# Two transformer blocks in float32 on one core: the second block's residual held by features, its norm scales applied behind the matmuls

## The reference

```python
def rmsnorm(x, g):
    x32 = x.astype(jnp.float32)
    y = x32 * lax.rsqrt(jnp.mean(x32 * x32, axis=-1, keepdims=True) + RMS_EPS)
    return (y * g.astype(jnp.float32)).astype(x.dtype)

def swiglu(h, w_gate, w_up, w_down):
    return (jax.nn.silu(h @ w_gate) * (h @ w_up)) @ w_down

def second_block(x, norm_mix, norm_ffn, w_qkv_a, w_out_a, sink_a, w_qkv_b, w_out_b,
              w_gate, w_up, w_down, norm_final):
    for i in range(DEPTH_2):
        h = rmsnorm(x, norm_mix[i])
        j = i // 2
        if i % 2 == 0:
            x = x + window_gqa_sink(h, w_qkv_a[j], w_out_a[j], sink_a[j])
        else:
            x = x + dilated_mixture_attention(h, w_qkv_b[j], w_out_b[j])
        h = rmsnorm(x, norm_ffn[i])
        x = x + swiglu(h, w_gate[i], w_up[i], w_down[i])
    return rmsnorm(x, norm_final)
```

## Time and profile before

| | us |
|---|---|
| median of 3 runs | 1625.37 |
| lowest and highest run | 1621.87 and 1625.46 |
| span of the profiled execution | 1619.0 |
| TensorE busy in it | 1377.1 (85%) |
| VectorE busy | 611.9 (38%) |
| ScalarE busy | 478.8 (30%) |
| DMA, mean over the span | 232 GB/s |

### The profile page before, as it was taken

How to read it: one execution, slowest core, us unless ns; L and a number is a source line. 1 busy time by engine, 2 the same in 40 slices (tenths; PEclk the granted TensorE clock), 3 DMA queues, 4 the chain that set the end, 5 groups by cost and what they waited for, 6 DMA issues and landing times.

```text
span 1619.0 us, 21195 instructions
## 1 busy us (share of the span) xinstructions
PE 1377.1 (85%) x8730; PEld 995.8 (62%) x8730; DVE 611.9 (38%) x848; ACT 478.8 (30%) x698; POOL 104.1 (6%) x99
## 2 busy tenths in 40 slices
PE   5999899786655655655699999999999999999997
PEld 1478665531111101111397899998999988899996
DVE  3225636410100100100447545455444455564544
ACT  2423522310000000000344534444344443343443
POOL 0000011100000000000034000000000045100000
PEclk9999999796767767767799999999999999999999
DMA  8443618989999999999641555655666620256562
GB/s 342 151 117 85 226 42 320 409 322 409 410 410 410 410 410 410 409 410 410 226 143 54 157 181 182 195 170 167 193 185 185 181 89 14 78 153 186 170 205 66
DMA packets 136658, 376.08 MB, mean 232 GB/s; under 512 B 8312, under 2 KB 55849, under 8 KB 136400
## 3 DMA queue, kind: packets, MB, share of 16 engines
q1 hardware_dynamic: 134600, 372.89, 65.0%
q10 hardware_dynamic: 1992, 2.26, 0.4%
HBM read 374.07 MB, written 1.05 MB: 232 GB/s over the span
## 4 chain that ended last, share of the span: by engine, by line
PE 68%; DMA 18%; DVE 6%; SPq 5%; ACT 2%; issue 1%; DVEq 0%; ACTq 0%
PE psum L1738 15%; PE psum L1739 15%; PE psum L1740 15%; DMA ring<-in_w_up 6%; DMA ring<-in_w_down 6%; DMA work<-in_w_gate 5%; SPq L528 5%; PE psum L2025 4%; PE psum L2143 3%; PE psum L2110 2%; PE psum L2123 1%; PE psum L1900 1%; PE psum L2105 1%; PE psum L1759 1%; PE psum L1893 1%
## 5 line engine op out<-in xcount | busy, mean ns | idle before, releaser
L1738 PE MATMUL psum<-parts 128*128 128x256 f32 (+1 forms) x1520 | 466.8, 307 | 3.7 <-DVE parts L1471 1.9
L1739 PE MATMUL psum<-parts 128*128 128x256 f32 (+1 forms) x1520 | 466.1, 307 | 0.0
L1740 PE MATMUL psum<-parts 128*128 128x256 f32 (+1 forms) x1520 | 465.8, 306 | 0.0
L1426 DVE TENSOR_TENSOR parts<-ring,parts 128x1024 fp32r<-128x1024 f32 x232 | 282.5, 1226 | 219.5 <-ACT parts L962 219.5
L962 ACT CAST parts<-ring 128x1024 fp32r<-128x1024 f32 x232 | 241.0, 1047 | 277.1 <-PE psum L1740 242.4
L1738 PEld LDWEIGHTS psum<-parts 128*128 128x128 f32 x1520 | 290.3, 191 | 18.8 <-issue 3.3
L1740 PEld LDWEIGHTS psum<-parts 128*128 128x128 f32 x1520 | 290.3, 191 | 13.3
L1739 PEld LDWEIGHTS psum<-parts 128*128 128x128 f32 x1520 | 290.4, 191 | 12.9
L2025 PE MATMUL psum<-ring,work 128*32 128x512 f32 x512 | 90.6, 846 | 64.8 <-DMA ring<-in_w_up 32.7
L2025 PE MATMUL psum<-work 128*32 128x512 f32 x512 | 85.7, 812 | 41.5 <-DMA work<-in_w_gate 21.7
L952 ACT ACTIVATE work<-psum 128x1024 f32<-128x1024 f32 x4 | 4.1, 1024 | 389.5 <-PE psum L2025 389.5
(11 more groups left out here) (315 smaller groups left out, 1483.4 us busy)
## 6 DMA issues: line engine op xcount, KB each, us to landing
ring<-in_w_qkv_b SPq DMA_DIRECT2D x72, 512.0 KB, 3.7
work<-in_w_gate SPq DMA_DIRECT2D x16, 2048.0 KB, 23.8
ring<-in_w_up SPq DMA_DIRECT2D x16, 2048.0 KB, 24.0
ring<-in_w_ada SPq DMA_DIRECT2D x48, 512.0 KB, 8.5
work<-in_w_down SPq DMA_DIRECT2D x12, 2048.0 KB, 24.0
ring<-in_w_gate SPq DMA_DIRECT2D x44, 512.0 KB, 3.9
ring<-in_w_up SPq DMA_DIRECT2D x44, 512.0 KB, 4.6
ring<-in_w_down SPq DMA_DIRECT2D x44, 512.0 KB, 3.6
```

Source lines behind the costliest of these rows:

```text
L1426: dve.tensor_tensor(part_of(lo_slots, t, n), ring[:, slot_2(t), 0:n], part_of(hi_slots, t, n), ALU.subtract).then_inc(lo_ready, 1)
L1738: pe.matmul(out, lhsT[0], rhs[0], start=start, stop=False, skip_group_check=True)
L1739: pe.matmul(out, lhsT[0], rhs[1], start=False, stop=False, skip_group_check=True)
L1740: return pe.matmul(out, lhsT[1], rhs[0], start=False, stop=stop, skip_group_check=True)
```

## The change

The residual of the second block is now `xT`, the same memory as `xres`, with features on partitions and tokens in the order that attention wants (even tokens, then odd). No stage turns it. The norm's factor per token, `r`, is not applied to the activations: `h_hi` and `h_lo` are x times the gain alone, and `r` multiplies results: q and k when they leave PSUM, v per partition, and in the FFN both the gate sums (before SiLU) and the product. `r` itself comes from squares on ScalarE, a sum over the eight feature tiles on VectorE (a reduction whose inner index steps by 256 elements), a matmul with ones that sums over the partitions, root and reciprocal of 256 elements. Where tokens are on partitions (v), `r` is turned by two small matmuls (`r_to_tokens`). The two norms at the start are one pass: `r_one` of the first, `r_all` the product.

The output projections and the first FFN's down projection are by features now, and their sums join `xT` bank by bank (`grow`). The second FFN's down projection stays by tokens: 16 matmuls (`residual`) put the turned residual into its sums first, and the final norm reads PSUM. The experts' results are added by features, for which x is turned once behind the router's logits. The Q weights come before the K weights. Three, not two, weight tiles are split before a stage's residual is added.

```diff
-            turn(xn, xt_ready)
+            gate(5)
...
+            turn(xn, xt_ready, X_BANK)
...
+            turn(xres, xt_ready, X_BANK)
             pe.wait_ge(aff_ready, 1)
...
-            gate(5)
             pe.wait_ge(top_done, 1)
...
+            def sums_of_squares(m, n=L):
+                pe.wait_ge(sq_summed, m + 1)
+                pe.matmul(ps[0][:, 0:n], ones, sq_sum[:, 0:n], start=True, stop=True).then_inc(sums_out, 1)
+
+            def r_to_tokens(m):
+                pe.wait_ge(r_ready, m + 1)
                 for t in range(TT):
...
+                    ins = pe.matmul(ps[1][:, 2 * t:2 * t + 2], r_all[:, P * t:P * t + P], ident[:, 0:2], start=True, stop=True)
+                ins.then_inc(sums_out, 1)
...
+                for k in range(KD):
+                    if k % 2 == 0:
+                        pe.wait_ge(o_lo_ready, o_ready + k // 2 + 1)
+                    w = weights(t + k)
+                    for f in range(KD):
+                        ins = feature_sums(w, bank, f, k, k == 0, k == KD - 1)
+                        if k == KD - 1 and f in (1, 3, 5):
+                            ins.then_inc(first_sums, 1)
+                    ins.then_inc(tiles_done, 1)
...
+                    for j in range(2):
+                        w = weights(t + j, turn)
+                        for f in range(KD):
+                            ins = products(ps[f // 2][:, L * (f % 2):L * (f % 2) + L], each(w, slice(None), slice(P * f, P * f + P)),
+                                           each(hid, slice(None), j), first and j == 0 and f % 2 == 0, last and j == 1)
...
+                def residual():
+                    for p in range(TT):
+                        for f in range(KD):
+                            pe.matmul(ps[2 * p + f // 4][:, P * (f % 4):P * (f % 4) + P], xT[:, f, P * p:P * p + P],
+                                            ident[:, :], start=(f % 4 == 0), stop=False, skip_group_check=True)
...
+                if i == 1:
+                    pe.wait_ge(r_tok_ready, 2)
...
+            def grow_and_norm(n, bank, done, gain):
+                grow(n, bank, done, 0)
+                grow(n, bank, done, 1)
+                dve.wait_ge(x_grown, 4 * n + 1)
+                low_h(n + 1, gain, 0)
+                grow(n, bank, done, 2)
+                dve.wait_ge(x_grown, 4 * n + 2)
+                low_h(n + 1, gain, 1)
+                grow(n, bank, done, 3)
...
+            def over_features(i, sq):
+                return dve.tensor_reduce(sq_sum[:, L * i:L * i + L], sq.rearrange("p k l -> p l k"), AX.X, ALU.add)
...
+            def rows_of_r(m, n):
+                dve.wait_ge(sums_out, (2, 5)[n])
+                dve.tensor_copy(r_tok[:, :], ps[1][:, 0:2 * TT]).then_inc(r_tok_ready, 1)
...
+                def block_gate(ready, buf):
+                    dve.wait_ge(tiles_done, ready)
+                    dve.tensor_tensor(gated_r[:, buf].rearrange("p (j l) -> p j l", j=2),
+                                      ps[4 + 2 * buf].rearrange("p (j l) -> p j l", j=2), by_r(2), ALU.mult).then_inc(ff_gate, 1)
...
+            def squares():
                 act.activation(stats[:, 90:91], ident[:, 0:1], ACT.Sqrt)
...
+                    ins = act.activation(sq_x[:, 2 * b:2 * b + 2, :], xT[:, 2 * b:2 * b + 2, :], ACT.Square)
```

More of the change, by code:

```diff
@@ new lines, in _ @@
+            for k in range(4, KD):
+                split(T_QA + k)
+            root(0)
+            split(T_KA)
+            root(1)
+            for t in range(T_KA + 1, T_OA):
+                split(t)
+            act.wait_ge(k_n_spread, 1)
+            act.copy(k_a[:, 2:4, :], ps[1]).then_inc(k_a_ready, 1)
+            act.wait_ge(tiles_done, T_VA + 2)
+            act.wait_ge(r_tok_ready, 1)
+            for t in range(TT):
+                ins = act.activation(v_a[:, t, :], ps[3][:, L * t:L * t + L], ACT.Copy, scale=r_tok[:, 2 * t:2 * t + 1])
@@ L1077, in _ @@
+            ins.then_inc(v_a_ready, 1)
             attention(0, T_OA)
-            for k in range(2):
+            for k in range(3):
                 split(T_FF[0] + k)
-            rms(4, x_grown, 1)
-            split(T_FF[0] + 2)
-            scaled(1, C_FFN2, halves)
+            normed(cols[:, C_FFN2:C_FFN2 + KD], x_grown, 0)
+            split(T_FF[0] + 3)
+            squares().then_inc(squared, 1)
             ffn(0, T_QB)
-            rms(5, x_grown, TT + 1)
-            split(T_QB + 2)
@@ L1086, in _ @@
-            scaled(2, C_MIX2 + KD, even_odd)
-            for i in range(3 * GROUPS):
-                for k in range(3 if i == 0 else 0, KD):
+            normed(cols[:, C_MIX2 + KD:C_MIX2 + 2 * KD], x_grown, 4)
+            split(T_QB + 3)
+            squares().then_inc(squared, 1)
+            for k in range(4, KD):
+                split(T_QB + k)
+            root(3)
+            for i in range(1, 3 * GROUPS):
+                for k in range(KD):
                     split(T_QB + KD * i + k)
-                    if k == 2:
-                        proj_half(i - 1)
+                    if k == 2 and (i - 1) % 3 == 2:
+                        values_out(i - 1)
@@ L1093, in _ @@
             attention(1, T_OB)
[L1094 removed]
+            for k in range(3):
                 split(T_FF[1] + k)
[L1096 to L1098 removed]
+            normed(cols[:, C_FFN2 + KD:C_FFN2 + 2 * KD], x_grown, 8)
+            split(T_FF[1] + 3)
+            squares().then_inc(squared, 1)
             ffn(1, None)
[L1100 removed]
+            act.activation(stats[:, 90:91], ident[:, 0:1], ACT.Sqrt)
```

577 lines of the change are left out of this document (300 added, 277 removed).

## The result

The changed kernel takes 1643.71 us (median of 4, 1641.04 to 1647.73) against 1625.41 for the kernel before on the same chip: a ratio of 1.0122, interval 1.0101 to 1.0144. It is slower by 18 us where 8 us less was forecast, and lies outside the range of 1613 to 1626. The profiled execution of the changed kernel spans 1645.9 us.

A forecast was written before the change was run, and what follows sets the result against it. TensorE was taken to bound the second block, the experts' weights by DMA the time before 792 us. Terms -4.8 - 2.8 - 0.8 + 6.1 - 0.9 - 2.2 - 2.8 = -8.2 us gave 1617.2, range 1613 to 1626.

The forecast's parts named there:

- (f): Start of the second block: first matmul 7.9 us earlier, most given back, including 2.0 for uncovered softmax latency; -0.9 us.
- (g): Routing: FFN gate moved into an idle stretch, clock taken as held at 1.00, first new expert load earlier; -2.2 us.
- (i): Remaining edits priced at nothing, among them the experts' sums as 8 x 256 columns, under DMA but for the last.
- (a): Boundaries one to three: TensorE resumes 1.35 us after the last matmul instead of pausing 6.86; bounds 0 and 2.5.
- (b): Norm's scale beside the matmuls: reduction 2.2 us, reciprocal 1.6, about 0.55 lost to the ones matmul; boundary one -4.8 us.
- the rival of half-rate reads: Reduction's strided reads at half rate, 4.4 us, make weights' low halves late: 5.0 us, total 1622.2; chance 0.15.
- the third rival: The same reduction costs more, turning the kernel slower from 6 us; at 7.2 us +19, 1636; chance 0.07.
- (c): Boundary two pays 2.1 us for r in token order after the eighth tile, -2.8; boundary three adds the residual, -0.8.
- (d): Output projections and first FFN's down projection: 38 tiles of 24 narrower matmuls at 2.88 instead of 2.72 us; +6.1 us.
- (e): Inside the FFN: extra VectorE operations and SiLU's wait cost nothing, under a cover of 1.6 us per block.
- (h): Tail after the last matmuls: 5.95 us instead of 8.75, since the addition goes; -2.8 us.
- the first rival: The clock falls in the FFN gate at 297.7; routing +1.6 instead of -2.2, total 1621.0; chance 0.25.

The follow-up runs named there:

- experiments 1 to 3: Changed kernel, ten unused matmuls before attention: 1612.12 us; kernel before, scores behind second value tile: 1660.96 us profiled; changed kernel, twenty unused matmuls behind fourth attention unit: 1623.18 us.
- experiment 7: Changed kernel with the sums over feature tiles reading their elements in a row instead of 1 KB apart: 1.12 ns an element; no total time given.
- experiment 9: Changed kernel with scores earlier, large tiles aligned, x transposes later, three additions for the reduction, r turned after the sixth tile: 1596.59 us against 1625.59 before.
- experiment 6: Changed kernel with scores behind the second value tile's first quarter and work put back to 416 bytes past a multiple of 512: 1618.79 us against 1625.59 before.
- experiment 2: Kernel before with the first scores moved behind the second value tile: profiled 1660.96 us; other executions 1657.71, 1652.27 and 1626.27 us.

## Why the prediction was wrong, point by point

- **(f) is the step that failed.** It named the stretch ("no longer covers softmax latency, 2.0") and sized it well (2.32 us), but priced only the idle time. The clock's part is 32.6 us (experiments 1 to 3). Terms (f) and (g) did ask about the clock, at a cold start and at the gate; here it was not asked. From the earlier trace rows term (g) reads that in attention the clock "stays at 1.00 once there", and takes it as a comfort; the runs show that a fall stays too. No rival had this mechanism. The rest of (f) holds: 8.0 us sooner at the first matmul (7.9 forecast), 6.5 given back (7.0); the half clock lasts from the first matmul (793.6) to 798.0, which is worth some 2 us, as summed.
- **(i) was the second miss, the other way.** "At nothing" was said of the experts' stage after looking at its instructions. Two small tiles moved a large one, and the DMA rate went from 410 to 420 GB/s: -11.1 us in this stage, 10.0 of them between its first and last landing. Without it the changed kernel would be near 1655. No rival had it.
- **(a)** Pause at boundaries 1.67 us from start to start, so some 1.55 over the normal step, forecast 1.35, all three the same: right. The rival that pauses stay at 4 us has fallen.
- **(b)** The reciprocal takes 1.75 us (1.6 forecast). The reduction takes 3.93, not 2.2: the lower bound was taken, and the rival of half-rate reads had the better duration (4.4) at a price of 5.0 us. TensorE waited 0.43 us for it at three places, and 0.50 at the FFN's first output; FFN and boundary two together are 1.4 over the sum, where experiment 7 gives back 1.6. Replacing it in experiment 9, with the move at boundary two, was worth 5.2 us. The slower reductions of the third rival didn't occur.
- **(c)** The wait behind the eighth tile came as told, 1.54 us: VectorE's copy of r, then the split behind it. The stretch is 0.7 over. Here too the clock was not asked: it fell behind this wait in five of nine profiles, for 1.4 us each (experiment 6), though not in that of the result.
- **(d)** 2.88 to 2.89 us a tile, as forecast. **(e)** No wait of 0.5 us or more in the later blocks: hidden, as forecast. **(h)** FFN and tail come to +2.7 instead of +1.9.
- **(g)** The gate ran at full clock from 302.3 to 306.5, but the clock fell behind it, in the pause ahead of the normed tokens: the transposes take 3.32 us, the logits 5.07, the transposes of x 3.65. That is the first rival's mechanism, a step later. The gain of 2.2 is not there (+1.9 in this pair, none over all variants).
- **The sum without the two misses.** -8.2 forecast, -7.0 measured in experiment 6 (interval -3.9 to -10). The total agrees; its parts do so less. In the changed kernel's table the second block without the attention comes to -3.5 where its terms gave -6.0, and over all profiles routing gains nothing where (g) gave -2.2. So part of the agreement is luck.
- **The signs.** Two of the prediction's own signs of being wrong came true: the reduction takes over 3 us, and the first new load goes out at 345.7 (7.1 of that is the first stretch's spread). Neither is what made the kernel slower.
- **The 6.4 us** between the median and the span were chance: the profiled execution of the kernel before was a fast one. In the other runs the time and the span of one execution differ by 1.8 to 2.2 us.

## What to carry to other kernels

Before a cover is taken from an idle stretch of TensorE, ask what the clock does behind it: if narrow matmuls follow, a fall can be paid over all of them (here 32.6 us), and ten useless dense matmuls are cheaper (2.3 us). When a change adds or resizes any tile, compare the start addresses of the large tiles that DMA fills, modulo 256 bytes, and the GB/s of a full stage, before the difference is given to the change. Cut both traces at the same events and read the clock column of each stretch; busy shares hide a halved clock.

## What the runs showed of the hardware that was not expected

- TensorE idle for 2.20 to 2.33 us at clock 1.00 ahead of attention was followed by 0.50 in all five profiles with such a stretch; by its time, one unprofiled execution of experiment 2 escaped it. Attention's units stay at 0.50 for some 70 us, though TensorE is busy throughout; 20 matmuls of 512 columns lift the clock, and without them it rose in the last outputs or the turning of the results (918.1 in experiment 2, 910.7 in the changed kernel). The Trainium skill (TensorE: Matmul & The Clock Gate, HAM oscillation — how this bites in real kernels) describes the fall behind waits for DMA, ahead of matmuls that recover each time; here the work behind did not recover for 72 us.
- An idle stretch of 1.55 us between dense matmuls was followed by 3.4 us at 0.50 in five of nine profiles, one of 1.85 us in none of four.
- 2 MB in rows of 4 KB from DRAM: 5.12 us if the rows start 128 or 416 bytes past a multiple of 512 in SBUF, 4.85 to 5.02 at a multiple of 256. With work and early alone well placed, loads into them take about 4.93 and into ring and tokens 5.1; with all tiles so, all take 4.97.
- A reduction over elements 1 KB apart takes 1.92 ns an element on VectorE, in a row 1.12.
